# Hybrid encoder layer on one core: the output projection's first pass taken in quarters, its tokens loaded through the result and row buffers

## What is computed

```python
mixed = jnp.concatenate([o_a.astype(h.dtype), o_b.astype(h.dtype), o_c.astype(h.dtype)], axis=-1)
return h + mixed @ w_out.astype(h.dtype)
```

## Time and profile before

| | |
|---|---|
| Median of 3 runs | 2594.44 us |
| Lowest and highest | 2594.44 and 2596.92 us |
| Profiled execution, its own time | 2589.97 us |
| Its span | 2588.3 us |
| TensorE busy | 2282.7 us, 88% of the span |
| ScalarE, VectorE, GpSimd busy | 28%, 43%, 15% |
| Output stage, from SyncE's first load to the end | 2190.01 to 2588.3 us |

### The profile page before, as it was taken

One profiled execution on the slowest core, in us unless ns is written; L12 is line 12 of the kernel. 1 busy time (PEld: TensorE's weight loads), 2 busy tenths in 40 slices (PEclk: granted clock), 3 DMA queues, 4 the chain that ended last, 5 costly groups with the idle time before them and its releaser, 6 DMA issues. The chain is left out here.

```text
span 2588.3 us, 31160 instructions
## 1 busy us (share of the span) xinstructions
PE 2282.7 (88%) x12032; PEld 1909.6 (74%) x12032; DVE 1107.8 (43%) x1682; ACT 717.0 (28%) x1160; POOL 397.0 (15%) x251
## 2 busy tenths in 40 slices
PE   6999999999999999994399998999956765599998
PEld 6788888888888888883288887888943433488887
DVE  7844444443441122212355554555427665322222
ACT  5411111111111011100345554444234344311111
POOL 3200000000000000000455554554000000000000
PEclk9999999999999999997699999999968897799999
DMA  7322222222222222211301221220050121544442
GB/s 234 133 98 73 73 73 73 73 73 73 73 72 73 73 73 73 73 49 36 119 26 63 74 74 58 74 74 17 9 166 25 53 66 63 200 150 143 144 143 86
DMA packets 74063, 220.02 MB, mean 85 GB/s; under 512 B 7488, under 2 KB 25024, under 8 KB 69744
## 3 DMA queue, kind: packets, MB, share of 16 engines
q1 hardware_dynamic: 63136, 179.35, 20.8%
q0 software_dynamic: 10832, 39.39, 4.0%
HBM read 174.02 MB, written 44.70 MB: 85 GB/s over the span
## 5 line engine op out<-in xcount | busy, mean ns | idle before, releaser
L73 PE MATMUL pr_acc<-x_hi,pr_w_lo 128*128 128x512 f32 (+1 forms) x1760 | 675.8, 384 | 25.9 <-DVE pr_w_lo L386 23.3
L75 PE MATMUL pr_acc<-x_hi,pr_w_hi 128*128 128x512 f32 (+1 forms) x1760 | 674.3, 383 | 0.0
L74 PE MATMUL pr_acc<-x_lo,pr_w_hi 128*128 128x512 f32 (+1 forms) x1760 | 674.2, 383 | 0.0
L73 PEld LDWEIGHTS pr_acc<-x_hi,pr_w_lo 128*128 128x128 f32 x1760 | 334.2, 190 | 91.6 <-issue 18.3
L74 PEld LDWEIGHTS pr_acc<-x_lo,pr_w_hi 128*128 128x128 f32 x1760 | 334.3, 190 | 63.8 <-issue 0.2
L75 PEld LDWEIGHTS pr_acc<-x_hi,pr_w_hi 128*128 128x128 f32 x1760 | 334.1, 190 | 63.6
L314 ACT ACTIVATE pr_w_hi<-pr_w_raw 128x1024 fp32r<-128x1024 f32 x118 | 124.8, 1059 | 758.4 <-PE pr_acc L75 739.3
L464 DVE TENSOR_TENSOR pr_padded<-pr_acc,pr_rstd 128x512 f32<-128x512 f32 x80 | 55.2, 692 | 501.5 <-PE pr_acc L75 501.3
L73 PE MATMUL ou_acc<-ou_w_hi,ou_m_lo 128*128 128x512 f32 x512 | 200.0, 391 | 46.8 <-ACT ou_w_hi L1678 46.8
L74 PE MATMUL ou_acc<-ou_w_lo,ou_m_hi 128*128 128x512 f32 x512 | 199.8, 390 | 0.0
L75 PE MATMUL ou_acc<-ou_w_hi,ou_m_hi 128*128 128x512 f32 x512 | 199.7, 390 | 0.0
(11 more groups left out here) (217 smaller groups left out, 2917.5 us busy)
## 6 DMA issues: line engine op xcount, KB each, us to landing
pr_w_raw<-in_w_in SPq DMA_DIRECT2D x118, 512.0 KB, 4.9
ou_w_raw<-in_w_out SPq DMA_DIRECT2D x32, 1024.0 KB, 4.8
proj_scratch<-pr_res POOLq DMA_DIRECT2D x51, 512.0 KB, 5.0
dl_qk<-proj_scratch SPq DMA_DIRECT2D x8, 1024.0 KB, 4.9
dl_grow<-gate_rows SPq DMA_DIRECT2D x8, 1024.0 KB, 7.3
dl_brow<-gate_rows SPq DMA_DIRECT2D x8, 1024.0 KB, 10.2
ou_w_raw<-mixed_scratch SPq DMA_DIRECT2D x16, 512.0 KB, 4.7
ou_x_in<-in_x SPq DMA_DIRECT2D x8, 1024.0 KB, 7.4
```

The source lines that it names most:

```text
L73: pe.matmul(out, w_lo, x_hi, start=first, stop=False)
L74: pe.matmul(out, w_hi, x_lo, start=False, stop=False)
L75: return pe.matmul(out, w_hi, x_hi, start=False, stop=last)
```

## The change

- Raw token tiles no longer lie over `w_raw` but over `res` and `x_in`: two slots in each, still four in all.
- SyncE issues four token tiles, weight quarter 0, four tiles, weight quarter 1, and so on. Quarters 0 and 1 wait for nothing; quarters 2 and 3 wait, as before, for VectorE's low part of quarters 0 and 1. The first load of `x_in` waits for the last token tile to be subtracted.
- ScalarE and VectorE take four token tiles and then the weight quarter, four times. ScalarE's first slice is written out, and its loop begins at the second.
- TensorE waits before quarter `q` of the first step for 4(q+1) token tiles, and no longer for 16 at its start.

The numbers and shapes of transfers and of arithmetic instructions are unchanged.

```diff
-        m_raw = w_raw[:].rearrange("p b q n -> p (b q n)").rearrange("p (b s) -> p b s", s=SEQ)
+        m_raw = [part for buf in (res, x_in) for part in
+                 (buf[:, 0:2].rearrange("p a n -> p (a n)"), buf[:, 2:4].rearrange("p a n -> p (a n)"))]
...
         @block.sync
         def _(sp):
-            for f in range(FT):
-                if f >= 4:
-                    sp.wait_ge(m_l, f - 3)
-                sp.dma_start(m_raw[:, f % 4], mixed[f]).then_inc(l_m[f % 4], 16)
+            def tokens(q):
+                for f in range(QUART * q, QUART * q + QUART):
+                    if f >= 4:
+                        sp.wait_ge(m_l, f - 3)
+                    sp.dma_start(m_raw[f % 4], mixed[f]).then_inc(l_m[f % 4], 16)
...
             def step(i, g, first):
 
                 for q in range(NQ):
-                    if first and q < 2:
-                        load(i, q, lambda: sp.wait_ge(m_l, FT))
-                    else:
-                        load(i, q, lambda: sp.wait_ge(w_l, i * (2 * NQ) + (g * NQ + q - 1)))
-                if not first:
+                    if first:
+                        tokens(q)
+                    load(i, q, lambda: None if first and q < 2 else
+                         sp.wait_ge(w_l, i * (2 * NQ) + (g * NQ + q - 1)))
+                if first:
+                    sp.wait_ge(m_l, FT)
+                else:
                     sp.wait_ge(o_r, i * (2 * GROUP) + g * GROUP)
...
         @block.scalar
         def _(act):
-            for f in range(FT):
-                act.wait_ge(l_m[f % 4], 16 * (f // 4 + 1))
-                act.activation(m_hi[:, f], m_raw[:, f % 4], ACT.Copy).then_inc(m_h, 1)
-            with act.Fori(0, NS) as i:
+            def high(i, g, q):
+                act.wait_ge(l_w[q % 2], i * (16 * NQ) + 16 * (g * (NQ // 2) + q // 2 + 1))
+
+                if q == 1:
+                    act.wait_ge(acc_done, i * (2 * GROUP) + (g * GROUP + ONE))
+                else:
+                    act.wait_ge(used, i * (2 * KU) + (g * KU + max(q - 1, 0) + ONE))
+                act.activation(w_hi[:, q % 2], w_raw[:, q % 2], ACT.Copy).then_inc(w_h, 1)
+
+            for q in range(NQ):
+                for f in range(QUART * q, QUART * q + QUART):
+                    act.wait_ge(l_m[f % 4], 16 * (f // 4 + 1))
+                    act.activation(m_hi[:, f], m_raw[f % 4], ACT.Copy).then_inc(m_h, 1)
+                high(0, 0, q)
+            for q in range(NQ):
+                high(0, 1, q)
+            with act.Fori(1, NS) as i:
                 for g in range(2):
                     for q in range(NQ):
...
+                        high(i, g, q)
...
         @block.vector
         def _(dve):
-            for f in range(FT):
-                dve.wait_ge(m_h, f + 1)
-                dve.tensor_tensor(m_lo[:, f], m_raw[:, f % 4], m_hi[:, f].bitcast(F32), ALU.subtract).then_inc(m_l, 1)
+            def tokens(q):
+                for f in range(QUART * q, QUART * q + QUART):
+                    dve.wait_ge(m_h, f + 1)
+                    dve.tensor_tensor(m_lo[:, f], m_raw[f % 4], m_hi[:, f].bitcast(F32), ALU.subtract).then_inc(m_l, 1)
...
+            tokens(0)
             low(0, 0, 0)
+            tokens(1)
             low(0, 0, 1)
 
             def step(i, g, first, last):
                 for q in range(2, NQ):
+                    if first:
+                        tokens(q)
                     low(i, g, q)
...
         @block.tensor
         def _(pe):
             pe.sem_inc(used, ONE)
             pe.sem_inc(acc_done, ONE)
-            pe.wait_ge(m_h, FT)
-            pe.wait_ge(m_l, FT)
-
-            def step(i, g, free):
+
+            def step(i, g, free, first=False):
                 for q in range(NQ):
+                    if first:
+                        pe.wait_ge(m_h, QUART * (q + 1))
+                        pe.wait_ge(m_l, QUART * (q + 1))
...
-            step(0, 0, True)
+            step(0, 0, True, True)
             step(0, 1, True)
```

## The result

| | before | after |
|---|---|---|
| Median of 4 runs | 2594.44 us | 2566.97 us |
| Lowest and highest | 2593.74 and 2596.92 us | 2565.92 and 2575.5 us |
| Profiled execution, its own time | 2589.97 us | 2575.5 us |
| Its span | 2588.3 us | 2573.9 us |
| SyncE's first token load to first matmul | 41.15 us | 14.19 us |

The ratio is 0.9900, with a 95% interval of 0.9885 to 0.9914. The forecast was 2568.2 us and 1.0% faster.

What follows compares the result with a forecast made beforehand. TensorE's start was taken to bound the output stage: first matmul at 2204.95 instead of 2231.16 gains 26.2 us, other terms taken as no difference, so 2594.44 - 26.2 = 2568.2 us, range 2562 to 2577.

Steps and rivals of the forecast that it cites:

- The bound: Output stage: TensorE's 46.8 us wait before its first matmul is its only one; an earlier start moves the end equally.
- Weight quarter 0 landed behind tile 3: DMA loads at the stage's start: quarter 0 lands 2.47 us behind tile 3, at 2200.5.
- rival 2: First weights land late, sharing with tiles 4 and 5 or more: gain 23 us, 2571 us; chance 0.08.
- The prediction's edge of 14.3 us: Lower end of the forecast 14.3 to 17.5 us from SyncE's first issue to the first matmul; central value 14.9.
- The roundings and the start: Weight quarter 0: ScalarE's high part 1.92 us, VectorE's low part 2.29 us, TensorE starts 0.15 us behind.
- The clock's spell: TensorE's first matmuls at 1.2 GHz for 3.5 us as before; quarter 0 takes 12.75 us, no difference taken.
- Feeding: TensorE stays fed at quarter borders: margins 5.3, 6.7 and 6.6 us for quarters 1, 2 and 3.
- Rival 1: TensorE waits at quarter borders, restarting at low clock: 6 to 26 us gained, in the middle 2580 us; chance 0.08.
- The sum: Whole kernel: 26.2 us off the median 2594.44 gives 2568.2 us, 1.0% faster.
- Rivals 3 and 4: 3: TensorE's clock stays down, 2604.6 us; 4: its start still hangs on the last tile, 2594 us; chance 0.02 each.
- One sign of being wrong: TensorE's first matmul past 2208 us would make the forecast wrong.
- The Trainium skill's figure: HBM loads limited to about 358 GB/s per core: quarter takes 2.93 us, gain 25.8 us; forecast kept the trace's 411 to 419.

Runs made afterwards that it cites:

- the 12-tile wait: The changed kernel with TensorE waiting for 12 token tiles instead of 4 before its first matmul; median 2579.88 us, ratio 0.9942.
- the changed kernel's third: A third profile of the changed kernel, no edit; 2571.62 us (one run), 15.79 us from first token load to first matmul.
- clock lifted: The changed kernel with 14 constant matmuls on TensorE, begun when the third token tile is rounded; median 2568.22 us, ratio 0.9901.
- the halves kernel: The changed kernel with its first four token tiles split by token halves, weight quarter 0 between first and second halves; median 2569.36 us, ratio 0.9905.
- the changed kernel's second profile: The changed kernel run again without edit; median 2568.84 us, ratio 0.9904, 14.30 us from first token load to first matmul.

## Why the prediction held

- **The bound.** The head stood on the path and nothing behind it did. Shown: the rest is 357.1 to 358.5 us for heads from 14 to 41 us, with the order of the tiles changed or not, and the 12-tile wait lengthened the stage by its full length.
- **Weight quarter 0 landed behind tile 3**, 2.49 us where I took 2.47. Sharing with later loads, the reason for rival 2, is hardly there in the changed kernel: when the quarter's last packet ends, 515 and 528 token packets are done in the first two profiles, and its first four tiles have 512. The head came out at 14.2 to 14.3 us against 14.94, since the tiles landed 1.28 us apart from the first one on (7.3 us for tile 3 against 8.04 in the profile of before, where tile 1 was 0.5 us late). The prediction's edge of 14.3 us was too tight: with weights in time for ScalarE to go on at 2199.11, its own rows give a start at 2199.11 + 1.92 + 2.29 + 0.15 = 2203.5, a head of 13.5 and a gain of 27.7, not 26.8. In three of the five profiles that have the quarter behind tile 3 of four whole ones (the changed kernel's third, 12 tiles, clock lifted) it came 1.6 us later, behind tiles that were late themselves. The packets show one engine behind the rest: in all three the last token packets start 0.16 us apart, one after the other, up to 8.3 us behind the first issue, where the others end at 6.7 to 6.8, and the quarter's first packets start at 6.5 to 6.6 in all five. So the term has a spread of its own, a head of 14.2 to 15.9, that the one profile of before couldn't show. Rival 2 had put up to 3 us on a late quarter; it was 1.6, and from the tiles ahead, not those behind.
- **The roundings and the start**: 1.91, 2.29 and 0.15 us, as in the rows.
- **The clock's spell**: 0.50 for 3.6 us, then 0.98 and 1.00; quarter 0 took 13.1 us, 0.3 more than before. The spell lasted 3.1 to 6.1 us among the kernels that have no wait in the rest, and the rest 357.06 to 358.45 us, so "no difference" has a spread of 1.4 us.
- **Feeding.** The margins that I had worked out were 5.3, 6.7 and 6.6 us. ScalarE's and VectorE's rows of the first step after:

```profile
2220.01 1.92 ACT L1677 ACTIVATE ou_w_hi<-ou_w_raw 128x2048 fp32r<-128x2048 f32 x1 [1.46 <-DMA ou_w_raw<-in_w_out]
...
2229.65 1.92 ACT L1677 ACTIVATE ou_w_hi<-ou_w_raw 128x2048 fp32r<-128x2048 f32 x1 [1.43 <-DMA ou_w_raw<-in_w_out]
...
2240.40 1.92 ACT L1677 ACTIVATE ou_w_hi<-ou_w_raw 128x2048 fp32r<-128x2048 f32 x1 [4.59 <-PE ou_acc L75]
2251.28 1.92 ACT L1677 ACTIVATE ou_w_hi<-ou_w_raw 128x2048 fp32r<-128x2048 f32 x1 [8.96 <-PE ou_acc L75]
```

```profile
2221.96 2.29 DVE L1710 TENSOR_TENSOR ou_w_lo<-ou_w_raw,ou_w_hi 128x2048 fp32r<-128x2048 f32 x1 [1.17 <-ACT ou_w_hi L1677]
...
2231.60 2.29 DVE L1710 TENSOR_TENSOR ou_w_lo<-ou_w_raw,ou_w_hi 128x2048 fp32r<-128x2048 f32 x1 [2.12 <-ACT ou_w_hi L1677]
...
2242.35 2.29 DVE L1710 TENSOR_TENSOR ou_w_lo<-ou_w_raw,ou_w_hi 128x2048 fp32r<-128x2048 f32 x1 [3.92 <-ACT ou_w_hi L1677]
```

ScalarE's row at 2240.40 is released by TensorE's end of quarter 1, and the next follows 10.88 us later, so quarter 0 ended near 2240.40 - 10.88 = 2229.5. VectorE had quarter 1's part at 2224.25, 5.3 us ahead of that. Quarter 2's part is there at 2233.89, due 2240.4: 6.5. Quarter 3's is there at 2244.64, due 2251.3: 6.6. One detail was otherwise: quarter 2's rounding (2229.65) was released by its load, which stands behind tile 11, 0.1 us after TensorE had left the slot: the load was there 27.4 us behind the first issue, where I had put 26. Rival 1's price for a wait, its own length and a restart at the low clock, was seen in the halves kernel (3.7 and 1.6 us). For this kernel rival 1 needed loads and roundings one after the other, and they overlapped.
- **The sum**: 26.2 us forecast; 26.6 in the stage's own profile (371.7 against 398.3), 27.5 and 26.5 between medians. Rivals 3 and 4 did not come up. One sign of being wrong that I had named did: the first matmul is past 2208 us, at 2216.40. It was given as a time of the profile of before, and the stage began 12.2 us later; behind SyncE's first issue it would have been 18.0 us, and 14.2 was measured.
- **The Trainium skill's figure.** While HBM feeds the head, the 13 slices from 2197 us of the changed kernel's second profile (the lower of the two rows above) are at 377 to 475 GB/s, 425 in the mean, and the mean over the whole of the first profile's head is 366. By "DMA: Bandwidth & Descriptors", section "Where 436 GB/s comes from", the rate would have stopped at 358. The Trainium skill's "HBM Reference", section "Specifications (TRN2)", says that a core streaming alone gets about 425, and the trace agrees with that one.

## What to carry to other kernels

A stage that loads everything before its first matmul can be judged from two rows, TensorE's first wait and the number of later ones; if there are none later, each microsecond off the first comes off the end, as long as the feeding engines' cost per piece stays under TensorE's. When pieces are made smaller, look at whether the DMA engines still finish together (their busy share in the last stretch before the landing) and at who frees the slots: half tiles brought no earlier start, and a late slot gave TensorE a second wait and a second low spell of its clock. Compare such a stage by its own start and end when the stages ahead of it vary by more than the effect.

## What the runs showed that I had not expected

- With half tiles the weight quarter landed no sooner, though the median packet of 2 KB was only 5% slower by the byte than one of 4 KB (84 and 159 ns). The 16 DMA engines didn't finish together: for the last 2.4 us before the landing they were 13% busy. The half tiles were ready 0.74 to 2.41 us apart, the whole ones 1.28.
- The same straggling came without any change of code: in three of five profiles one engine was 1.6 us behind the others at the end of tile 3, and the head that much longer.
- In the one profile where the queue ran dry it came back slowly: with weight quarter 0 moved back, the rate was 139 and 115 GB/s for 1 us and 197 to 385 for the next 3.5, and the quarter landed 2.6 us later than by its place.
- The same code ahead of the stage ended anywhere between 2190.0 and 2202.2 us, with a granted clock of 0.89 down to 0.82 over the 245 us ahead of 2190. What decides it is open.
